# Experts in two parts with separate gate and value passes, and a fourth first-round place of 64 tokens

## The chip, the core and the metric

The kernel runs on one core of one Trainium2 chip. The metric is the device time of one execution in microseconds, as the median of several runs; lower is better. The instructions of PE (matmuls), ACT, DVE, POOL and SP (which here only issues DMAs) run side by side and wait for each other by semaphores.

## What is computed

A two-layer backbone over 256 latent tokens and 256 context tokens, with 1024 channels, all in float32. The last sub-layer, which the change touches, is a top-2-of-8 expert SwiGLU with 3584 hidden columns for each expert:

```python
logits = jnp.einsum('btd,de->bte', h, router_w)
top_vals, top_idx = lax.top_k(logits, 2)
gates = jax.nn.softmax(top_vals, axis=-1)
for e in range(8):
    g, u = jnp.split(h @ w_in[e], 2, axis=-1)
    out = out + combine[..., e:e + 1] * ((jax.nn.silu(g) * u) @ w_out[e])
```

`w_in[e]` is 1024 x 7168 and `w_out[e]` is 3584 x 1024. A row of `w_in` in memory is 28 KB: 14 KB of gate columns, then 14 KB of value columns. The weights of one expert are 42 MiB, those of all eight 336 MiB, and each is read once.

## The kernel before

Everything up to the router is left as it is by the change. The expert stage is `experts(rnd)` in each engine's program. `rnd` 0 is the round that always runs. It takes the experts one after the other at eight places; a place has room for 96 tokens (`CAP`), or for 64 (`SMALL`) at the places in `SMALL_PLACES`. DVE's `expert_order` ranks the experts by their number of tokens, expert 0 always counts as the fullest and stands at place 0, and the least loaded stand at the small places. If an expert has more tokens than its place holds, `overflow_flag` sets a flag, and rounds 1 and 2 run as well, each over all eight experts.

**Blocks and the ring.** SP's `fetch` brings the weights in blocks of 1 MiB, in the order of the list `ROUND`, into a ring of 18 slots (`RING0`). SP issues block n when PE has counted block n - 18 as used (`used`). All transfers stand in one queue. An expert is cut into four steps over its hidden columns, `WIDTH = [1024, 1024, 1024, 512]`. A block of an input step holds, for 128 of the 1024 input rows, 1024 gate and 1024 value columns: two rows of 4 KB in each partition. The fourth step's input blocks hold two times 128 input rows with 512 gate and 512 value columns, in two DMAs: rows of 2 KB. A block of an output step has 256 rows of `w_out`, which lie one behind the other: 8 KB for each partition (in the fourth step two rows of 4 KB). So an expert is 24 input blocks of 4 KB rows, 4 of 2 KB rows, 12 output blocks of 8 KB rows and 2 of 4 KB rows, 42 in all. The list interleaves them: input step s, output step s - 1, and so on, with the first input step of the next expert ahead of the last output step.

**PE.** `in_block` holds the tokens of one input slice as weights, 32 tokens in each of the array's four column groups, and streams the block's columns through; the array's four groups work side by side. With 96 tokens the three groups of 32 tokens take three column groups, and the fourth takes a share of the other columns, so that a 1 MiB block is 12 quarter-array matmuls of 512 columns' worth. With 64 tokens it is 8. The program has one line for most of these matmuls, L1141. Between blocks PE also does `transposes` (of the activated hidden values, 128 x 128 each, L1636 to L1648), `gather` (the next expert's tokens by a one-hot product), `combine` (the last expert's rows back to their tokens) and a transpose of the one-hot (L1707).

**ACT and DVE.** After each input step ACT's `silu` reads the gate from PSUM bank 0 (and a share of bank 2), DVE's `product` multiplies by the value of bank 1, PE transposes the result, and ACT's `transposed` copies the transposed values to SBUF for the output blocks. `hte` copies the gathered tokens, `yhi` and `ylo` split an expert's result for the combining product, `accumulate` adds it up.

The rule for an input block, and what the transfer of a block waits for:

```python
if s_ < STEPS - 1:
    rows = expert_in_w[0, e, b * P:(b + 1) * P, :].rearrange("p (u n) -> p u n", u=2)
    sp.dma_start(w, rows[:, :, 1024 * s_:1024 * s_ + 1024]).then_inc(done, 16)
...
sp.wait_ge(used, B_MOE + n - RING0 + 1)
```

Of the kernel before, what the change touches and what calls it, by code (L numbers as in the profile page):

```python
# [39 lines left out]
SMALL_PLACES = (1, 4, 7)  # L40
N_SMALL = len(SMALL_PLACES)
STEPS = 4
WIDTH = [1024, 1024, 1024, 512]
# [23 lines left out]
def step_blocks(kind, s_, ahead=0):  # L67
    return [(kind, s_, b, ahead) for b in range(WIDTH[s_] // (128 if kind == "in" else 256))]


HEAD = step_blocks("in", 0)
LAST = []
for s_ in range(1, STEPS):
    LAST += step_blocks("in", s_) + step_blocks("out", s_ - 1)
CYCLE = LAST + step_blocks("in", 0, 1) + step_blocks("out", STEPS - 1)
LAST = LAST + step_blocks("out", STEPS - 1)
EB = len(CYCLE)
ROUND = HEAD + CYCLE * (NE - 1) + LAST
assert EB % RING == 0 and len(ROUND) == NE * EB
# [4 lines left out]
def capacity(rnd, e):  # L84

    return SMALL if rnd == 0 and e in SMALL_PLACES else CAP

# [67 lines left out]
def backbone(nc, x, c, ctx_in, c_ctx, ada_w, ada_b, norm_g, mix_in_w, mix_out_w, win_sink, diff_qkv_w,  # L155
# [52 lines left out]
    def area(*specs):  # L208
# [14 lines left out]
    (WMOE, HTE, YS, PTR, YACC, ONEHOT, SIL) = area(  # L223
        ("w_moe", [P, 2 * SPL, BLK], F32), ("h_te", [P, DK, CAP], F32), ("y_split", [P, 2, D], F32R),
        ("onehot_t", [P, 2 * P], F32R), ("y_acc", [P, XT, D], F32), ("onehot", [P, XT, CAP], F32),
        ("silu_g", [P, 768], F32))
# [3 lines left out]
    ACTN = RES[:, 3, 0:768]  # L230
# [48 lines left out]
    ACTT = work(10240, 2, 768)  # L279
# [11 lines left out]
    ps = stack.enter_context(nc.psum_tensor("ps", [P, 8, 512], F32))  # L291

# [199 lines left out]

    def slot_of(rnd, n):
        return LATER[n % RING] if rnd else n % RING0
# [9 lines left out]
    def moe_parts(n):  # L504
        return 2 if ROUND[n][:2] == ("in", STEPS - 1) else 1

    def moe_landed(rnd, e, n):

        def count(top, size):
            return sum(16 * moe_parts(m) for m in range(n % size, top, size))  # L510
        if rnd == 0:
            return count(n + 1, RING0)
        first = sum(16 * moe_parts(m) for m in range(slot_of(rnd, n), len(ROUND), RING0))
        return first + (rnd - 1) * count(len(ROUND), RING) + \
            e * (count(8 + 2 * EB, RING) - count(8 + EB, RING)) + count(n + 1, RING)

    def moe_view(rnd, n):

        kind, s_ = ROUND[n][:2]
        w = ring(slot_of(rnd, n))  # L520
        if kind == "out":
            return w.rearrange("p (j n) -> p j n", j=2)
        if s_ < STEPS - 1:
            return w.rearrange("p (u n) -> p u n", u=2)
        return w.rearrange("p (k u n) -> p k u n", k=2, u=2)
# [11 lines left out]
    def _(sp):  # L537
# [29 lines left out]
        def fetch(rnd, e, n, order=None):  # L567

            kind, s_, b, ahead = ROUND[n]
            w, done = moe_view(rnd, n), w_landed[slot_of(rnd, n)]  # L570
            e = e + ahead if ahead else e
            e = order[e] if order else e
            if kind == "out" and s_ < STEPS - 1:
                rows = expert_out_w[0, e, 1024 * s_ + 256 * b:1024 * s_ + 256 * b + 256, :]
                sp.dma_start(w, rows.rearrange("(p j) n -> p j n", j=2)).then_inc(done, 16)
            elif kind == "out":
                rows = expert_out_w[0, e, 1024 * s_ + 256 * b:1024 * s_ + 256 * b + 256, :]
                sp.dma_start(w, rows.rearrange("(j p) n -> p j n", p=P)).then_inc(done, 16)
            elif s_ < STEPS - 1:
                rows = expert_in_w[0, e, b * P:(b + 1) * P, :].rearrange("p (u n) -> p u n", u=2)  # L580
                sp.dma_start(w, rows[:, :, 1024 * s_:1024 * s_ + 1024]).then_inc(done, 16)
            else:
                for u in range(2):
                    rows = expert_in_w[0, e, 2 * b * P:(2 * b + 2) * P, ED * u + 1024 * s_:ED * u + ED]
                    sp.dma_start(w[:, :, u, :], rows.rearrange("(k p) n -> p k n", p=P)).then_inc(done, 16)  # L585

        def refill(rnd, e, n, turns=0):

            sp.wait_ge(used, moe_base(rnd) + turns * EB + max(n - RING + 1, 0))
            fetch(rnd, e, n)  # L590

        def experts(rnd):
            if rnd == 0:
                for n in [5, 6, 7, 8, 0, 1, 2, 3, 4] + list(range(9, RING0)):
                    if n == 0:
                        sp.wait_ge(scores, U0 + U1)
                    elif n == 3:
                        sp.wait_ge(pv_done, U0 + U1)
                    elif 5 <= n < 5 + RAW:
                        was, j = raw_order[N_RAW - RAW + n - 5]  # L600
                        assert was == "w"
                        sp.wait_ge(lo_done, j + 1)
                    elif n == 5 + RAW:
                        sp.wait_ge(used, B_DOUT + 2)
                    elif n == 7 + RAW:
                        sp.wait_ge(used, B_MOE)
                    elif n == RING0 - 1:
                        sp.wait_ge(hn_done, XT)
                    fetch(0, 0, n)
            else:  # L610
                for n in range(RING):
                    refill(rnd, 0, n)
            if rnd == 0:
                order = [0]
                for n in range(RING0, len(ROUND)):
# [4 lines left out]
                    fetch(0, (n - 8) // EB, n, order)  # L620
                return
            with sp.Fori(0, NE - 2) as e:
                for n in range(RING, EB + 8):
                    refill(rnd, e, n, e)
                for n in range(8, RING):
                    refill(rnd, e + 1, EB + n, e)
            for n in range(RING + EB * (NE - 2), len(ROUND)):
                refill(rnd, (n - 8) // EB, n)
# [88 lines left out]
    def _(act):  # L717
# [310 lines left out]
        def experts(rnd):  # L1028
# [12 lines left out]
            def step_end(s_):  # L1041
                return 8 + max(n for n, x in enumerate(LAST) if x[:2] == ("in", s_)) + 1

            def silu(e, s_, ahead=0):
                J = STEPS * NE * rnd + e * STEPS
                h, q = WIDTH[s_] // 2, WIDTH[s_] // 4
                if s_:
                    act.wait_ge(used, base + e * EB + step_end(s_))
                else:
                    act.wait_ge(used, base + e * EB + 8 - ahead)  # L1050
                act.wait_ge(act_done, FG + J + s_)
                if capacity(rnd, e) == SMALL:
                    act.activation(SIL[:, 0:h], ps[:, 0, 0:h], ACT.Silu).then_inc(silu_done, 1)
                    return
                ins = act.activation(SIL[:, 0:h], ps[:, 0, 0:h], ACT.Silu)  # L1055
                if rnd == 0 and isinstance(e, int) and e + s_ == 0:
                    ins.then_inc(silu_half, 1)
                act.activation(SIL[:, 512:512 + q], ps[:, 2, 0:q], ACT.Silu).then_inc(silu_done, 1)  # L1058

            def transposed(e, s_):  # L1060
                J = STEPS * NE * rnd + e * STEPS
                act.wait_ge(tr_ready, J + (s_ + 1))
                if capacity(rnd, e) == SMALL:
                    n = 4 * P if s_ < STEPS - 1 else 2 * P
                    act.activation(ACTT[:, s_ % 2, 0:n], ps[:, 5, 0:n], ACT.Copy).then_inc(actt_ready, 1)
                elif s_ == STEPS - 1:
                    act.activation(ACTT[:, s_ % 2, 0:384], ps[:, 5, 0:384], ACT.Copy).then_inc(actt_ready, 1)
                else:
                    act.activation(ACTT[:, s_ % 2, 0:512], ps[:, 5, :], ACT.Copy)
                    act.activation(ACTT[:, s_ % 2, 512:768], ps[:, 6, 0:256], ACT.Copy).then_inc(actt_ready, 1)  # L1070

            def yhi(e, last):
                act.wait_ge(used, base + e * EB + 8 + len(LAST if last else CYCLE))
# [6 lines left out]
            def cycle(e, last=False):  # L1080
                transposed(e, 0)
                silu(e, 1)
                transposed(e, 1)
# [3 lines left out]
                silu(e, 2)  # L1087
                transposed(e, 2)
                silu(e, 3)
                if not last:  # L1090
                    hte(NE * rnd + e + 2, capacity(rnd, 0 if rnd else e + 1))
                transposed(e, 3)
# [5 lines left out]
                if not last:  # L1098
                    silu(e + 1, 0, len(step_blocks("out", STEPS - 1)))
# [3 lines left out]
            silu(0, 0)  # L1103
# [35 lines left out]
    def _(pe):  # L1139
# [405 lines left out]
        def in_block(kk, w, width, hold=None):  # L1545

            h, q_ = width // 2, width // 4
            first, last = kk == 0, kk == DK - 1
            for u in range(2):
                if hold:  # L1550
                    hold(u)
                for tg in range(3):
                    mm(ps[group(tg), u, 0:h], HTE[:, kk, group(tg)], w[:, u, 0:h], first, last)
                mm(ps[group(3), u, 0:h], HTE[:, kk, group(0)], w[:, u, h:width], first, last)
            if hold:
                hold(2)
            for u in range(2):
                for n, (tg, c_) in enumerate(QUARTERS):
# [851 lines left out]
```

## Time and profile before

| | |
|---|---|
| median of 3 runs | 1689.19 us (1688.94 to 1690.8) |
| span of the profiled execution | 1685.4 us |
| PE busy in the span | 1612.0 us (96%) |
| DVE, ACT busy | 526.0 us, 400.6 us |
| bytes moved by DMA | 474.61 MB |
| largest group of DMAs | expert weights, 1024.0 KB each |

The profiled execution has no time of its own beside its span; the median lies 3.8 us above the span, and that much is taken to lie around every span of this kernel. The expert stage begins at about 822 us of the span, when PE gathers the first expert's tokens, and goes on to its end. Matmuls are pipelined and their ends are modelled, so a busy PE in a table says little; whether PE waits is read from the chain of waits and from the starts of its matmuls.

### The profile page before, as it was taken

What the parts mean: (1) busy time and instruction counts of PE and PEld (TensorE: products, weight loads), DVE (VectorE), ACT (ScalarE), POOL (GpSimd) and SP (SyncE); (2) the same over time, 40 slices, a digit from 0 to 9 for tenths busy, and PEclk for the clock granted to TensorE, in tenths of its full rate; (3) what the DMA queues carried; (4) which work ended last, traced back from release to release, by engine and by line L of the source; (5) the groups of instructions that cost most, each with busy time, mean ns of one, the idle gap of its engine ahead of it and who ended that gap; (6) DMA issues with size and microseconds to landing.
All of it is one profiled execution on the core that took longest, in us unless ns stands there. A gap on an engine that the chain in (4) does not pass through costs nothing.

```text
span 1685.4 us, 31518 instructions
## 1 busy us (share of the span) xinstructions
PE 1612.0 (96%) x13979; PEld 963.8 (57%) x13979; DVE 526.0 (31%) x829; ACT 400.6 (24%) x724; POOL 34.4 (2%) x70
## 2 busy tenths in 40 slices
PE   5999989999999989998899999999999999999995
PEld 2855778878788877866545334454453444544432
DVE  3427467665433366367400010101101010020012
ACT  3327342222132253357300101011011100010101
POOL 1000100010000000000000000000000000000000
PEclk9999999999999999999899999999999999999998
DMA  9661816576533324214799999999999999999995
GB/s 367 206 225 41 255 45 200 200 254 246 201 100 110 105 79 149 77 50 180 292 376 386 372 409 409 413 406 411 409 408 413 398 411 402 409 412 399 410 400 229
DMA packets 140559, 474.61 MB, mean 282 GB/s; under 512 B 11176, under 2 KB 35144, under 8 KB 121984
## 3 DMA queue, kind: packets, MB, share of 16 engines
q1 hardware_dynamic: 137344, 467.64, 72.9%
q0 software_dynamic: 3072, 4.88, 1.1%
q8 instruction: 112, 1.84, 0.4%
q14 instruction: 31, 0.25, 0.0%
HBM read 471.36 MB, written 1.13 MB: 280 GB/s over the span
## 4 chain that ended last, share of the span: by engine, by line
PE 89%; DVE 4%; DMA 3%; ACT 1%; SPq 1%; issue 1%; DVEq 0%; ACTq 0%
PE ps L1141 86%; DMA w_raw<-in_ada_w_dram 1%; DMA w_moe<-in_expert_out_w_dram 1%; SPq L585 1%; PE ps L1648 1%; PE ps L1324 1%; DVE work L1832 1%; DVE row_max L2100 1%; DVE w_lo L1763 0%; DVE p L2126 0%; PE ps L1640 0%; ACT p L956 0%; DVE h_t L1821 0%; DVE work L2030 0%; PE ps L1485 0%
## 5 line engine op out<-in xcount | busy, mean ns | idle before, releaser
L1141 PE MATMUL ps<-w_hi,h_t 128*128 128x512 f32 (+1 forms) x960 | 294.2, 387 | 11.5 <-DVE h_t L1821 5.4
L1141 PE MATMUL ps<-h_t,w_hi 128*128 128x512 f32 (+1 forms) x768 | 223.1, 375 | 6.2 <-DVE h_t L1821 6.2
L1141 PEld LDWEIGHTS ps<-w_hi,h_t 128*128 128x128 f32 x960 | 180.4, 190 | 48.9 <-DVE w_lo L1946 4.1
L1763 DVE TENSOR_TENSOR w_lo<-w_raw,w_hi 128x2048 fp32r<-128x2048 f32 x57 | 130.5, 2291 | 228.2 <-ACT w_hi L726 227.8
L1141 PE MATMUL ps<-w_lo,h_t 128*128 128x512 f32 (+1 forms) x480 | 185.3, 386 | 0.0
L726 ACT ACTIVATE w_hi<-w_raw 128x2048 fp32r<-128x2048 f32 x57 | 108.9, 1913 | 301.5 <-PE ps L1141 301.3
L1141 PE MATMUL ps<-w_raw,h_te 128*32 128x512 f32 (+2 forms) x2224 | 178.4, 474 | 1.5 <-ACT silu_g L1055 0.8
L1141 PE MATMUL ps<-w_moe,h_te 128*32 128x512 f32 (+2 forms) x2256 | 170.5, 456 | 0.0
L1141 PEld LDWEIGHTS ps<-h_t,w_hi 128*128 128x128 f32 x768 | 141.9, 192 | 33.8 <-issue 9.2
L1141 PE MATMUL ps<-work 128*32 128x512 f32 (+6 forms) x1232 | 147.9, 485 | 6.7 <-ACT p L956 3.7
L2286 DVE TENSOR_TENSOR residual<-silu_g,ps 128x512 f32<-128x512 f32 (+1 forms) x20 | 12.4, 621 | 436.9 <-ACT silu_g L1058 418.0
L1141 PE MATMUL ps<-work,h_te 128*32 128x256 f32 (+1 forms) x1744 | 144.3, 483 | 2.8 <-DMA work<-in_expert_in_w_dram 2.2
L1141 PE MATMUL ps<-h_t,w_lo 128*128 128x512 f32 (+1 forms) x384 | 143.8, 374 | 0.0
L1141 PEld LDWEIGHTS ps<-w_raw,h_te 128*32 128x32 f32 x2224 | 71.0, 110 | 104.8 <-issue 83.8
L1141 PEld LDWEIGHTS ps<-w_moe,h_te 128*32 128x32 f32 x2256 | 71.1, 110 | 91.9 <-issue 71.0
L1055 ACT ACTIVATE silu_g<-ps 128x512 f32<-128x512 f32 (+1 forms) x20 | 10.9, 544 | 398.2 <-PE ps L1141 398.2
L1141 PEld LDWEIGHTS ps<-work,h_te 128*32 128x32 f32 x1744 | 56.0, 110 | 86.1 <-issue 65.0
L1141 PEld LDWEIGHTS ps<-w_lo,h_t 128*128 128x128 f32 x480 | 91.5, 191 | 17.5
L1141 PEld LDWEIGHTS ps<-work 128*32 128x32 f32 (+3 forms) x1232 | 57.8, 126 | 75.3 <-issue 55.0
L1141 PE MATMUL ps<-w_moe,work 128*32 128x512 f32 (+1 forms) x1088 | 94.1, 493 | 0.3 <-DMA w_moe<-in_expert_out_w_dram 0.3
L1141 PE MATMUL ps<-w_raw,work 128*32 128x512 f32 (+1 forms) x832 | 81.4, 532 | 1.4 <-DMA w_raw<-in_expert_out_w_dram 1.3
L1141 PEld LDWEIGHTS ps<-h_t,w_lo 128*128 128x128 f32 x384 | 73.6, 192 | 12.6
(285 smaller groups left out, 1269.9 us busy)
## 6 DMA issues: line engine op xcount, KB each, us to landing
w_raw<-in_expert_in_w_dram SPq DMA_DIRECT2D x68, 1024.0 KB, 18.7
w_moe<-in_expert_in_w_dram SPq DMA_DIRECT2D x62, 1024.0 KB, 18.8
work<-in_expert_in_w_dram SPq DMA_DIRECT2D x53, 1024.0 KB, 18.7
w_raw<-in_ada_w_dram SPq DMA_DIRECT2D x48, 1024.0 KB, 5.6
w_raw<-in_expert_out_w_dram SPq DMA_DIRECT2D x37, 1024.0 KB, 17.9
w_moe<-in_expert_out_w_dram SPq DMA_DIRECT2D x36, 1024.0 KB, 18.0
work<-in_expert_out_w_dram SPq DMA_DIRECT2D x33, 1024.0 KB, 17.7
w_raw<-in_ffn_in_w_dram SPq DMA_DIRECT2D x44, 512.0 KB, 5.0
```

The lines of the kernel that those rows point to most:

```text
L585: sp.dma_start(w[:, :, u, :], rows.rearrange("(k p) n -> p k n", p=P)).then_inc(done, 16)
L726: act.activation(WHI[:, b % SPL, :], WRAW[:, slot_w[b], :], ACT.Copy).then_inc(hi_done, 1)
L1055: ins = act.activation(SIL[:, 0:h], ps[:, 0, 0:h], ACT.Silu)
L1141: return pe.matmul(out_, l, r, start=first, stop=last, skip_group_check=True)
L1324: ins = pe.transpose(ps[:, 4 + kv, c_ * P:(c_ + 1) * P], PR0[:, 2 * (u % 2) + kv, c_ * P:(c_ + 1) * P], ID[:])
L1648: ins = pe.transpose(ps[:, 5 + x // 4, 128 * (x % 4):128 * (x % 4) + 128], pairs[:, x // 2, x % 2, :], ID[:])
L1763: dve.tensor_tensor(WLO[:, b % SPL, :], WRAW[:, slot_w[b], :], WHI[:, b % SPL, :].bitcast(F32), ALU.subtract).then_inc(lo_done, 1)
L1832: ins = dve.tensor_scalar(TF[s][:, n % 2, 256 * k:256 * k + 256], ps[:, UNIT_BANK[s][st][u], 256 * k:256 * k + 256], ACOL[:, st, 2 * u + k ...
L2100: link(dve.tensor_reduce(MX[:, p:p + 2], ps[:, p ^ 2:(p ^ 2) + 2, :], AX_X, ALU.max))
L2286: ins = dve.tensor_tensor(ACTN[:, 0:h], SIL[:, 0:h], ps[:, 1, 0:h], ALU.mult)
```

## The change

An expert is now two parts, A with 2048 hidden columns and B with 1536. The gate columns of a part and its value columns are separate passes (GA, UA, GB, UB), each of eight blocks of 128 input rows: one row of 8 KB for each partition in part A (1 MiB), one of 6 KB in part B (0.75 MiB, which still takes a whole slot of the ring). The output blocks are as before, 8 of part A and 6 of part B; two of these have 4 KB rows where the place has 96 tokens, none where it has 64. So an expert is 46 blocks. The gate pass and the value pass use the same PSUM banks 0 to 2: ACT's `silu` reads the gate out of them before the value pass begins, and DVE's `product` reads the value before the next gate pass. The first-round places with 64 tokens are 1, 3, 5 and 7 instead of 1, 4 and 7. The activated values are multiplied in place, in a tile in `residual`.

```diff
-SMALL_PLACES = (1, 4, 7)
+SMALL_PLACES = (1, 3, 5, 7)
-STEPS = 4
-WIDTH = [1024, 1024, 1024, 512]
+HALVES = ("A", "B")
+WIDTH = {"A": 2048, "B": 1536}
...
+HEAD = in_pass("GA") + in_pass("UA")
+LAST = in_pass("GB") + out_blocks("A", 0, 4) + in_pass("UB") + out_blocks("A", 4, 8)
+CYCLE = LAST + in_pass("GA", 1) + out_blocks("B", 0, 3) + in_pass("UA", 1) + out_blocks("B", 3, 6)
+LAST = LAST + out_blocks("B", 0, 6)
...
-            elif s_ < STEPS - 1:
-                rows = expert_in_w[0, e, b * P:(b + 1) * P, :].rearrange("p (u n) -> p u n", u=2)
-                sp.dma_start(w, rows[:, :, 1024 * s_:1024 * s_ + 1024]).then_inc(done, 16)
...
+                c0 = (0 if what[0] == "G" else ED) + (0 if what[1] == "A" else 2048)
+                sp.dma_start(w, expert_in_w[0, e, b * P:(b + 1) * P, c0:c0 + WIDTH[what[1]]]).then_inc(done, 16)
...
+                n = act_columns(capacity(rnd, e), half)
+                act.activation(SIL[:, 0:n], PSF[:, 0:n], ACT.Silu).then_inc(silu_done, 1)
...
+            for b in range(3):
+                if hold:
+                    hold(b)
+                n = 512 if half == "A" or b < 2 else P
+                for tg in range(3):
+                    piece(tg, b, 0, n, tg, 512 * b)
+                if half == "A":
+                    ins = piece(3, b, 0, 512, b, 1536)
+                elif b == 0:
+                    piece(3, 0, 0, 256, 0, 1280)
+                    piece(3, 0, 256, 256, 1, 1280)
+                elif b == 1:
+                    piece(3, 1, 0, 256, 2, 1280)
+                    piece(3, 1, 256, P, 0, 1152)
+                    piece(3, 1, 384, P, 1, 1152)
+                else:
+                    ins = piece(3, 2, 0, P, 2, 1152)
...
+                if begin and what == "UA":
+                    freed = ((silu_half, 1), (silu_half, 2), (silu_done, FG + 1))
+                    hold = lambda bank: pe.wait_ge(*freed[bank])
...
+                elif b == 0 and what == "GA":
+                    pe.wait_ge(act_done, FG + J + 2 * ahead)
+                elif b == 0 and what == "UA":
+                    pe.wait_ge(silu_done, FG + J + 2 * ahead + 1)
```

SP's queue, in the first expert's last input step, before: rows of four DMAs with two rows of 512 columns in each partition (2 KB each), between output blocks with one row of 2048 (8 KB). `ISA` stands for what SP does for the wait.

```order
L575 DMA w_raw<-in_expert_out_w_dram 128x2048
L585 ISA
L585 DMA w_raw<-in_expert_in_w_dram 128x2x512
L585 ISA
L585 DMA w_raw<-in_expert_in_w_dram 128x2x512
```

Now, at the same place in an expert (the value pass of part B follows the first four output blocks of part A):

```order
L598 DMA w_moe<-in_expert_out_w_dram 128x2048
L601 ISA
L601 DMA w_moe<-in_expert_in_w_dram 128x1536
L601 ISA
L601 DMA w_moe<-in_expert_in_w_dram 128x1536
```

Each input DMA now has one unbroken row for each partition, of 1536 or 2048 columns, where it had two of 512 or 1024.

PE's matmuls of one 1 MiB block of the fourth step before, with 96 tokens (two input slices, each eight matmuls of 256 and eight of 128 columns):

```order
L1141 MATMUL ps<-w_extra,h_te 32x256 x8
L1141 MATMUL ps<-w_extra,h_te 32x128 x8
L1141 MATMUL ps<-w_extra,h_te 32x256 x8
L1141 MATMUL ps<-w_extra,h_te 32x128 x8
L1141 MATMUL ps<-onehot,h_nat 128x64 x16
```

And of one 0.75 MiB block of part B now, with the gather for the next expert behind it:

```order
L1140 MATMUL ps<-w_extra,h_te 32x512 x3
L1140 MATMUL ps<-w_extra,h_te 32x256 x2
L1140 MATMUL ps<-w_extra,h_te 32x512 x3
L1140 MATMUL ps<-w_extra,h_te 32x256
L1140 MATMUL ps<-w_extra,h_te 32x128 x6
L1140 MATMUL ps<-onehot,h_nat 128x64 x16
```

The fourth column group of the array now has two or three shorter matmuls in a row while the other three have one of 512 columns each; before, all four had matmuls of one length in turn.

ACT's first expert before, from the copy of the first transposes on:

```order
L1069 ACTIVATE work<-ps 128x512
L1070 ACTIVATE work<-ps 128x256
L1055 ACTIVATE silu_g<-ps 128x512
L1058 ACTIVATE silu_g<-ps 128x256
L1069 ACTIVATE work<-ps 128x512
L1070 ACTIVATE work<-ps 128x256
L1086 ACTIVATE onehot_t<-ps 96x256
L1055 ACTIVATE silu_g<-ps 128x512
L1058 ACTIVATE silu_g<-ps 128x256
```

And now, from the same copy on:

```order
L1072 ACTIVATE work<-ps 128x1536
L1066 ACTIVATE residual<-ps 128x1152
L1088 ACTIVATE onehot_t<-ps 96x256
L1047 ACTIVATE h_te<-ps,mod_cols,scale_cols 128x64 x8
L1072 ACTIVATE work<-ps 128x1152
L1066 ACTIVATE residual<-ps 128x1024
```

ACT reads up to three banks with one instruction, and has two silus and two copies for each expert where it had four of each.

## Rows read from the trace of the kernel before

**Rows 1.** The page: its first line, and DMA's share and rate in 40 slices.

```profile
span 1685.4 us, 31518 instructions
...
DMA  9661816576533324214799999999999999999995
GB/s 367 206 225 41 255 45 200 200 254 246 201 100 110 105 79 149 77 50 180 292 376 386 372 409 409 413 406 411 409 408 413 398 411 402 409 412 399 410 400 229
```

**Rows 2.** Stretches: busy time of each engine, granted clock, DMA share and rate.

```profile
core 0: us, PE busy (x) PEld busy (x) DVE busy (x) ACT busy (x) POOL busy (x), PEclk, DMA share, GB/s
...
1200.00:1300.00 100.00, 100.00 (x1215) 43.61 (x1211) 9.71 (x20) 10.59 (x26) 0.00 (x0) 1.00 1.02 408
...
940.00:950.00 10.00, 10.00 (x104) 3.19 (x100) 0.00 (x0) 0.00 (x0) 0.00 (x0) 1.00 0.96 370
...
1632.00:1668.00 36.00, 29.97 (x318) 11.09 (x310) 1.19 (x3) 3.05 (x6) 0.00 (x0) 1.00 0.89 350
```

**Rows 3.** PE's timeline, first expert: start us, length us, matmuls (two records each), idle before.

```profile
828.21 13.11 PE L1141 MATMUL ps<-work,h_te 128*32 128x512 f32 x160 [0.52 <-ACT h_te L1035]
841.13 7.92 PE L1141 MATMUL ps<-w_raw,h_te 128*32 128x512 f32 x96
849.86 5.37 PE L1141 MATMUL ps<-w_raw,h_te 128*32 128x512 f32 x64 [0.81 <-ACT silu_g L1055]
855.16 0.98 PE L1648 MATMUL ps<-ident,residual 128*128 128x128 f32 x6
...
871.58 2.76 PE L1141 MATMUL ps<-w_moe,work 128*32 128x512 f32 x32
...
915.18 7.98 PE L1141 MATMUL ps<-w_moe,h_te 128*32 128x256 f32 x192
...
925.70 3.78 PE L1141 MATMUL ps<-onehot,h_nat 128*128 128x64 f32 x32
...
940.37 1.90 PE L1141 MATMUL ps<-work,h_te 128*32 128x512 f32 x16
942.09 3.19 PE L1141 MATMUL ps<-w_raw,h_te 128*32 128x512 f32 x28
```

**Rows 4.** The chain that ended last, 1110 to 1400 us: start us, us, what.

```profile
1134.63 0.48 PE ps L1644 x3
...
1253.09 0.48 PE ps L1644 x3
```

**Rows 5.** The same chain, 1440 to 1460 us.

```profile
1452.93 0.48 PE ps L1644 x3
```

**Rows 6.** The same chain, 1600 us to the end.

```profile
1617.12 8.77 PE ps L1141 x80
...
1647.44 21.01 DMA w_moe<-in_expert_out_w_dram
1668.45 0.04 issue
1668.50 1.97 PE ps L1141 x16
```

**Rows 7.** DMA packets of 1460:1480, 1260:1280, 1160:1180, 1100:1120 us, in this order.

```profile
DMA packets 2109, 8.16 MB, mean 408 GB/s; under 512 B 124, under 2 KB 124, under 8 KB 2107
...
DMA packets 1710, 8.28 MB, mean 414 GB/s; under 512 B 125, under 2 KB 125, under 8 KB 1278
...
DMA packets 1631, 8.26 MB, mean 413 GB/s; under 512 B 125, under 2 KB 125, under 8 KB 1124
...
DMA packets 2153, 8.17 MB, mean 409 GB/s; under 512 B 158, under 2 KB 158, under 8 KB 1639
```

**Rows 8.** DMA packets of 12:24 us, while ada_w comes in 8 KB rows.

```profile
DMA packets 707, 5.10 MB, mean 425 GB/s; under 512 B 85, under 2 KB 85, under 8 KB 85
```

**Rows 9.** SP's DMA queue of 950:1668 us: packets, MB, share of 16 engines.

```profile
q1 hardware_dynamic: 72261, 289.86, 100.9%
```

**Rows 10.** ACT's and DVE's groups by form, 1120 to 1300 us: busy, mean ns, idle.

```profile
L1055 ACT ACTIVATE silu_g<-ps 128x512 f32<-128x512 f32 x3 | 1.8, 597 | 67.5 <-PE ps L1141 67.5
...
L2286 DVE TENSOR_TENSOR residual<-silu_g,ps 128x512 f32<-128x512 f32 x3 | 2.1, 686 | 68.6 <-ACT silu_g L1058 68.6
```

More of the change, by code:

```diff
@@ L1543, in group, with in_block, piece @@
             return slice(GROUP * tg, GROUP * tg + GROUP)
[L1545 to L1549, printed above, removed]
+        def in_block(half, k, w, hold=None):
+            first, last = k == 0, k == DK - 1
+            def piece(q, bank, c0, n, tg, w0):
+                return mm(ps[group(q), bank, c0:c0 + n], HTE[:, k, group(tg)], w[:, w0:w0 + n],
+                          first and c0 == 0, last)
+            for b in range(3):
@@ L1550, in in_block @@
                 if hold:
-                    hold(u)
+                    hold(b)
+                n = 512 if half == "A" or b < 2 else P
                 for tg in range(3):
[L1553 to L1557, printed above, removed]
-                for n, (tg, c_) in enumerate(QUARTERS):
-                    ins = mm(ps[group(n), 2, u * q_:u * q_ + q_], HTE[:, kk, group(tg)],
-                             w[:, u, h + c_ * q_:h + c_ * q_ + q_], first and u == 0, last)
@@ L1575, in out_block @@
-        def out_block(s_, m, w):
-            for j in range(2):
-                first = s_ == 0 and m == 0 and j == 0
-                last = s_ == STEPS - 1 and m == 1 and j == 1
-                for tg in range(3):
-                    mm(ps[group(tg), 3, :], hidden(s_, m, j, tg), w[:, j, 0:512], first, last)
-                mm(ps[group(3), 3, :], hidden(s_, m, j, 0), w[:, j, 512:1024], first, last)
-                for n, (tg, c_) in enumerate(QUARTERS):
-                    ins = mm(ps[group(n), 4, 0:256], hidden(s_, m, j, tg),
+                    piece(tg, b, 0, n, tg, 512 * b)
@@ new lines, in small_hidden, with out_block @@
+        def small_hidden(half, m, j, tg):
+            c_, x = m // (OUTS[half] // 2), m % (OUTS[half] // 2)
+            at = P * (tile_at(SMALL, half) + 2 * x + j) + 32 * (2 * c_ + tg)
+            return ACTT[:, at:at + GROUP]
+        def out_block(half, m, w):
+            for j in range(2):
+                first = half == "A" and m == 0 and j == 0
+                last = half == "B" and m == 5 and j == 1
+                for tg in range(3):
+                    mm(ps[group(tg), 3, :], hidden(half, m, j, tg), w[:, j, 0:512], first, last)
+                mm(ps[group(3), 3, :], hidden(half, m, j, 0), w[:, j, 512:1024], first, last)
+                for n, (tg, c_) in enumerate(QUARTERS):
+                    ins = mm(ps[group(n), 4, 0:256], hidden(half, m, j, tg),
@@ L1598, in small_out_block @@
[L1598 to L1607 removed]
+                    ins = mm(ps[group(n), 3, :], small_hidden(half, m, j, tg), w[:, j, 512 * c_:512 * c_ + 512],
@@ L1688, in cycle @@
+                for n in range(at, len(ROUND) if last else len(HEAD) + EB):
+                    kind, what, b, ahead = ROUND[n]
+                    if (what, b) == ("GA", 0):
                         pe.wait_ge(hte_ready, NE * rnd + e + 2)
-                    if (kind, s_, b) == ("out", 0, 0):
+                    if (what, b) == ("A", 0):
                         pe.wait_ge(acc_done, N * 4 + 1)
-                    product(0 if last else e, n, J, capacity(rnd, 0 if rnd else e + ahead))
-                    if (kind, s_, b) == ("in", 1, 1):
-                        transposes(e, 0)
@@ L1694, in cycle @@
-                    if (kind, s_, b) == ("in", 1, 4) and not (rnd == 0 and at == 8 and e == 0):
+                    product(e, n, capacity(rnd, 0 if rnd else e + ahead))
+                    if (what, b) == ("GB", 1):
+                        transposes(e, "A")
+                    if (what, b) == ("GB", 4) and not (rnd == 0 and not last and e == 0):
                         pe.wait_ge(y_lo, 17 * rnd + e * 2 + 1)
-                        pe.wait_ge(actt_ready, J + 1)
+                        pe.wait_ge(actt_ready, 2 * (NE * rnd + e) + 1)
@@ L1709, in cycle @@
-                    if last and rnd == 0 and (kind, s_, b) == ("out", STEPS - 2, 2):
+                    if (what, b) == ("A", 1):
+                        for t in range(XT):
+                            ins = pe.transpose(ps[0:cap, 7, t * P:(t + 1) * P], ONEHOT[:, t, 0:cap], ID[:])
+                        ins.then_inc(ptt_ready, 1)
+                    if (what, b) == ("UB", DK - 1) and not last:
+                        gather(NE * rnd + e + 2, capacity(rnd, 0 if rnd else e + 1))
+                    if (what, b) == (("A", 5 if early else 7) if last else ("GA", 1)):
+                        transposes(e, "B")
@@ L1710, in cycle @@
+                    if last and rnd == 0 and (what, b) == ("B", 1):
                         pe.wait_ge(gate_row, 1)
@@ L1714, in cycle @@
                         ins.then_inc(gate_spread, 1)
-                    if (kind, s_, b) == ("in", STEPS - 1, 3) and not last:
-                        pe.wait_ge(actt_ready, J + STEPS - 1)
-                        gather(NE * rnd + e + 2, capacity(rnd, 0 if rnd else e + 1))
             if rnd:
@@ L1723, in experts @@
                 pe.wait_ge(hte_ready, NE * rnd + 1)
-            for n in range(8):
-                if rnd == 0:
+            for n in range(len(HEAD)):
+                if rnd == 0 and n < DK:
                     pe.wait_ge(*((hte_first, n + 1) if n < DK - 1 else (hte_ready, 1)))
-                product(0, n, STEPS * NE * rnd, CAP)
+                product(0, n, CAP)
             if rnd:
```

349 lines of the change are left out of this document (149 added, 200 removed).

## The prediction, made before the changed kernel ran

> **What bounds the kernel now.** I read the page's slices first. From slice 21 on, the expert stage, DMA's share is 9 in every slice but the last, at around 408 GB/s [rows 1], and the table of stretches puts it at 1.02 of sixteen engines [rows 2]. PE reads as 100% busy there too, but ends of matmuls are modelled, so that settles nothing. The chain of waits does: from 828 us it goes along PE alone to 1617 and a little beyond, with no wait for a landing; then it turns to SP and the DMA queue, and the last block's landing at 1668.45 starts the last matmuls at 1668.50 [rows 3, 4, 6]. So both run nearly level. PE paces the stage until some 40 us before its end, the queue paces the rest, and the queue had been full all along. Whoever makes only PE faster gains nothing: the last landing stays at 1668.45.
>
> The queue's own account: in 950 to 1668 us it moved 289.86 MB, or 276.4 MiB [rows 9], so 59.6 of the 336 MiB were in at 950. In 940 to 950 it moved 370 GB/s, 3.5 MiB [rows 2]; at 940.37, when PE begins block 40 (the second expert's first, 64 tokens, [rows 3]), 56.1 MiB were in. Slots allow 58 at that moment. A block is thus in about 1.9 blocks, or 4.9 us, after its slot comes free. From there the queue never lacks a slot for long: block 57 is in at about 945.3, and the other 278 MiB take until 1668.45, 723.2 us, which is 109.25 us for an expert's 42 MiB.
>
> **What a packet costs.** Packets are as long as the rows. In 20 us sixteen engines have 320 us; I charge markers and instruction fetches to the data packets [rows 7]. The first stretch has 1983 packets of 4 KB: 0.1614 us each. The second has 1153 of 4 KB and 430 of 8 KB (two fetches taken off): (320 - 186.1) / 430 = 0.311; the third 999 and 505: 0.314; I take 0.313. The fourth has 512 of 8 KB and, by its bytes, 444 of 4 KB and 1037 of 2 KB: 0.0849. A packet costs some 0.01 us beside its bytes, so longer rows are cheaper for the byte. For 6 KB no row exists; it lies between 0.0849 + 0.1614 = 0.246 (cut in two) and 0.75 x 0.309 = 0.232, and I take the middle of 4 and 8 KB, 0.2372. That 8 KB rows with a gap between them (here 28 KB apart) go as fast as the unbroken output blocks is borne out by `ada_w`, whose 8 KB rows lie 24 KB apart: 622 packets in 192 engine-microseconds, 0.309, at 425 GB/s [rows 8].
>
> **The change part by part.** *Rows of the transfers.* Before, an expert is 6656 packets of 4 KB, 2048 of 2 KB and 1536 of 8 KB: 1074.3 + 173.9 + 480.8 = 1729.0, over 16 engines 108.06 us. The queue needed 109.25, 1.1% more. Now, with 96 tokens: 3584 of 8 KB, 2048 of 6 KB, 512 of 4 KB: 1121.8 + 485.8 + 82.6 = 1690.2, or 105.64 us; with 64 tokens 3840 and 2048: 105.48. With the same 1.1%, 106.7 us an expert: 2.5 us less for each.
>
> *The ring.* A 0.75 MiB block takes a whole slot, so the ring holds fewer bytes. PE begins block 16 at 871.58 before [rows 3]. Now blocks 0 to 15 are again of 1 MiB and 2.58 us (841.13 - 828.21 over five, [rows 3]). Blocks 16 to 18 are of part B, whose 96-token matmuls are three quarters of the columns, 1.94 us; with 12 transposes (0.92 us for six, so 1.84) block 18 is done at about 879.3. From there PE frees slots of 0.75 MiB every 1.94 us, and what is fetched into them is soon 1 MiB at 2.5 us: the queue is the slower one from block 36 on, where it was so only from block 57 before. Block 36 is in 4.9 us later, at 884.2, with 16 + 6 + 4 + 6 + 1 = 33 MiB. The other 303 MiB take 303 / 42 x 106.7 = 769.8: the last landing at 1654.0 instead of 1668.45. Of the 18 us that the rates would give, 4 go to the ring.
>
> *PE.* A cycle with 96 tokens takes 118.46 us (1134.63 to 1253.09, [rows 4]), one with 64 tokens beside one with 96 together 199.84 (1253.09 to 1452.93, [rows 4, 5]), so 81.4. The fourth small place replaces 118.5 by 81.4, 37 us of PE. Transposes are as many for a 96-token expert and cost some 0.5 us less in two sets than in four. PE now needs about 828.2 + 4 x 199 = 1624 without waits (some 4 less, since the last cycle has no gather), 30 before the last landing. So the fourth place gives nothing by itself: the work it removes is hidden behind the queue. Without it PE would need 37 more, 1661 less 4, about level with the queue.
>
> *New waits.* In the first expert UA follows GA directly and GB follows UA, in the same banks; each waits for one bank's silu or product, 0.81 us as at block 8 before [rows 3]. One of the two is new; the six transposes that stood before block 16, 0.92 us [rows 3], are gone from there, so block 16 keeps its 871.58. In the later experts at least three output blocks (5.2 us with 64 tokens) lie between the passes, over a silu or a product of 1536 columns, at most three times 0.6 or 0.69 us [rows 10]. PE's gather (3.7 us, [rows 3]) is followed by four output blocks, as before. Had a wait of 3 us for each pair of experts no cover, PE's 199 stay under the queue's 213.4. Blocks 0 and 1 now use slots that SP fills later, but all slots stood filled or issued before 828. The tail behind the last landing is the same.
>
> *The sum.* 1668.45 - 1654.0 = 14.5 us less. The span goes from 1685.4 to 1670.9, and with the 3.8 us around it the time is 1674.7; I say 1674.5.
>
> **A rule against it.** The stretches of 2, 4 and 8 KB rows differ in cost for the byte by 8% [rows 7]. The Trainium skill's page "DMA: Bandwidth & Descriptors" (Specifications) puts the least transfer for line rate at 512 B. By that, rows of 2 to 8 KB would all go at one rate, and the first rival below would be the outcome. The trace speaks against it within this range.
>
> **The rivals.** *One rate for all rows: slower.* If input rows of 8 and 6 KB, 28 KB apart, go at the rate of 4 KB rows, only the ring's smaller content is left: 303 MiB at 109.25 / 42 from 884.2 end at 1672.4, 4 us later than now, time 1693. It decides where an expert takes more than 108.7 us. Against it: [rows 8]. 6%.
>
> *Part B's matmuls do not pack.* The fourth column group has two or three matmuls in a row beside one in the others. If the others wait, a block costs up to 512 + 256, 512 + 256 and 128 column turns instead of 1152: about 2.8 us, 13.7 more in a 96-token expert. PE's pair then needs 213, as much as the queue's, and PE ends near 1624 + 55 - 4 = 1675, 4 us behind its end now (1670.47, [rows 6]): time 1693. The nearest row is the fourth step's, with 128- and 256-column matmuls at 2.63 us a MiB [rows 3], no dearer, but of equal lengths. It matters from about 2.4 us a block. 6%.
>
> *More than that: 8 KB rows at 0.309 and fewer fetches.* With [rows 8]'s price all through, an expert takes 104.3; with the 1.1% it is 105.4, the last landing at 1645, time 1665; without it 1657. 9%.
>
> *The clock.* Once small experts wait for the queue, PE works 1.72 us (942.09 - 940.37, [rows 3]) of each 2.5. If the granted clock fell to 1.2 GHz there, a block would take 3.44 us, over the queue's pace, and each such expert 50 us more: about 1775. Sixteen such MiB undo the gain. But in 1632 to 1668 us PE waited just so, for the same blocks, and the clock stood at 1.00 [rows 2], 2.4 GHz. The Trainium skill ("TensorE: Matmul & The Clock Gate", HAM oscillation) warns that waits for DMA throttle the array; this stretch does not show it. 3%.
>
> *Overflow.* Routing the reference's inputs gives 58, 55, 70, 77, 62, 65, 62, 63 tokens. Expert 0 is kept out; the four least of the rest, 55, 62, 62, 63, fit into 64. Were the fourth over 64, two more rounds of eight experts at 107 us would run, 1700 us. 2%.
>
> **How the numbers follow.** The forecast itself: 74%, between 1667 and 1682 (an expert at 105.5 to 108 us). The range takes part of the faster rival and reaches toward the slower two: 1664 to 1684.5. A change under 0.2%, 3.4 us, is about what a measurement cannot tell from none. Faster: 74 + 9 = 83%. A few of each rival that ends near 1693 fall within 0.2% (1692.6): 5%. Slower: 12%.
>
> **What will show it.** Stretches of GA and UA transfers should run at 415 to 420 GB/s, an expert's 44 MB should take 106.7 us, the chain should turn to the DMA queue near 1200 us and not at 1620, and PE should stand idle in the small experts while its clock stays 1.00. Part B blocks should start 1.94 us apart with 96 tokens. The last landing should be at 1654 and 17 us before the span's end. I would be wrong if the rate stays at 408, if blocks of part B take over 2.4 us, or if matmuls double in length behind waits.

## The result, and the profile after

| | before | after |
|---|---|---|
| median, four runs each on one chip | 1689.71 us | 1673.07 us (1671.87 to 1674.8) |
| ratio | 1 | 0.9903, 95% interval 0.9891 to 0.9914 |
| profiled execution: span, own time | 1685.4 us, not known | 1670.0 us, 1671.87 us |

The change makes the kernel 16.6 us faster in the medians and 15.4 in the profiled spans. 1674.5 was predicted, with a range of 1664 to 1684.5. All ratios leave out runs over 1.5% above the fastest of the same kernel, as a slow state; there were two, both of e6_two_dmas.

The page of the changed kernel, its span, DMA's share and rate in 40 slices, the packets and the chain by engine:

```profile
span 1670.0 us, 28575 instructions
...
DMA  9661816676523323213699999999999999999995
GB/s 368 210 226 36 258 51 202 199 256 231 217 85 120 117 82 126 101 51 138 253 318 390 417 418 421 417 419 418 418 421 418 419 418 418 420 418 419 418 418 213
DMA packets 106754, 474.42 MB, mean 284 GB/s; under 512 B 11176, under 2 KB 35144, under 8 KB 70784
...
PE 64%; SPq 19%; DMA 9%; DVE 5%; issue 2%; ACT 1%; DVEq 0%; ACTq 0%
```

Against [rows 1] the share in the expert stage still reads 9, in every slice but the last, and only the rate shows the change: from slice 24 on, but for the last, it is 417 to 421 GB/s where it wandered between 398 and 413. The digit says that the queue is never empty, not how fast it is. The chain that ends last now turns to the queue after two fifths of the stage, and from there on changes between the queue (SPq is SP's sequencer, which issues the transfers; DMA is a block under way) and PE. Its pieces from 1132 us on (start us, us, what):

```profile
1132.68 1.25 PE ps L1654 x9
1133.92 10.48 PE ps L1140 x96
1144.56 2.00 SPq L601
...
1242.07 26.44 DMA work<-in_expert_out_w_dram
1268.55 1.92 PE ps L1140 x16
1270.52 4.11 PE ps L1140 x36
...
1627.61 26.15 DMA w_raw<-in_expert_out_w_dram
1653.76 0.04 issue
1653.80 1.97 PE ps L1140 x16
```

In [rows 4] PE stood alone in it. The last landing was at 1668.45 [rows 6] and is at 1653.76. PE's waits, from 1140 to 1654 us (what waits for what, us in total, times, longest):

```profile
PE ps L1140 <- DMA w_raw<-in_expert_in_w_dram: 6.1, 14, 0.6
PE ps L1140 <- DMA work<-in_expert_out_w_dram: 5.0, 10, 0.7
PE ps L1140 <- DMA w_moe<-in_expert_in_w_dram: 4.4, 12, 0.4
PE ps L1140 <- DMA w_raw<-in_expert_out_w_dram: 3.0, 6, 0.6
```

They are many and short, nearly all of the small places' blocks; the longest one, a block of output weights in `w_moe`, is 1.0 us. And two stretches of the new kernel (the columns are those of [rows 2]), the second with a small place in it; PE is not quite full and its clock is:

```profile
1200.00:1300.00 100.00, 98.79 (x1024) 43.34 (x1020) 7.60 (x12) 9.10 (x15) 0.00 (x0) 1.00 1.01 419
...
1340.00:1440.00 100.00, 92.09 (x912) 32.71 (x908) 8.87 (x16) 9.43 (x19) 0.00 (x0) 1.00 1.01 418
```

### The profile page after: what moved, and what is told of

Same layout as the page of the kernel before. It is cut to its first block, busy times and chain, and to the rows that moved or that the text cites. A ratio compares the mean times of both kernels' runs of the same rounds, so it can differ in the third digit from the quotient of the medians.

```text
span 1670.0 us, 28575 instructions
## 1 busy us (share of the span) xinstructions
PE 1583.0 (95%) x12596; PEld 953.8 (57%) x12596; DVE 519.8 (31%) x791; ACT 391.1 (23%) x655; POOL 34.5 (2%) x70
## 4 chain that ended last, share of the span: by engine, by line
PE 64%; SPq 19%; DMA 9%; DVE 5%; issue 2%; ACT 1%; DVEq 0%; ACTq 0%
PE ps L1140 62%; SPq L601 13%; SPq L598 6%; DMA w_moe<-in_expert_out_w_dram 2%; DMA work<-in_expert_out_w_dram 2%; DMA w_raw<-in_expert_out_w_dram 2%; DMA work<-in_expert_in_w_dram 1%; DMA w_raw<-in_ada_w_dram 1%; DMA w_moe<-in_expert_in_w_dram 1%; PE ps L1323 1%; DVE work L1835 1%; PE ps L1654 1%; DVE row_max L2103 1%; DVE w_lo L1766 0%; SPq L596 0%
## 5 line engine op out<-in xcount | busy, mean ns | idle before, releaser
L2290 DVE TENSOR_TENSOR residual<-residual,ps 128x1152 f32<-128x1152 f32 (+3 forms) x15 | 19.4, 1292 | 529.1 <-PE ps L1140 529.1
L1140 PE MATMUL ps<-w_raw,h_te 128*32 128x512 f32 (+2 forms) x1694 | 159.5, 519 | 7.0 <-DMA w_raw<-in_expert_in_w_dram 6.1
L1140 PE MATMUL ps<-work 128*32 128x512 f32 (+6 forms) x1104 | 141.9, 498 | 11.4 <-DMA work<-in_expert_out_w_dram 5.0
L1140 PE MATMUL ps<-work,h_te 128*32 128x512 f32 (+2 forms) x1662 | 147.4, 506 | 0.9 <-ACT h_te L1047 0.5
L1140 PEld LDWEIGHTS ps<-w_raw,h_te 128*32 128x32 f32 x1694 | 61.3, 110 | 98.9 <-issue 70.2
L1140 PEld LDWEIGHTS ps<-work,h_te 128*32 128x32 f32 x1662 | 65.6, 110 | 78.8 <-issue 61.7
L1140 PEld LDWEIGHTS ps<-work 128*32 128x32 f32 (+3 forms) x1104 | 53.4, 128 | 79.0 <-issue 52.2
L1140 PE MATMUL ps<-w_raw,work 128*32 128x512 f32 (+1 forms) x1024 | 93.8, 513 | 3.0 <-DMA w_raw<-in_expert_out_w_dram 3.0
L1140 PE MATMUL ps<-w_moe,work 128*32 128x512 f32 (+1 forms) x832 | 76.2, 515 | 1.6 <-DMA w_moe<-in_expert_out_w_dram 1.6
L1140 PEld LDWEIGHTS ps<-w_raw,work 128*32 128x32 f32 x1024 | 34.3, 110 | 58.7 <-issue 42.9
```

Source lines behind the costliest of these rows:

```text
L1140: return pe.matmul(out_, l, r, start=first, stop=last, skip_group_check=True)
L2290: dve.tensor_tensor(SIL[:, 0:n], SIL[:, 0:n], PSF[:, 0:n], ALU.mult).then_inc(act_done, 1)
```

## The experiments

Eight kernels ran, each against the kernel before on its own chip. The ratio to the kernel before is what I compare: 0.001 of it is 1.7 us. The expert stage starts up to 5 us earlier or later in one profiled execution than in another, so places in two traces are compared after taking off that shift, read from one row: the start of the matmuls of block 8, behind the hold for ACT, at 850.09 in the changed kernel.

### Part A's rows cut in two (e4_cut_a), then both parts' (e3_cut_both)

```diff
-                sp.dma_start(w, expert_in_w[0, e, b * P:(b + 1) * P, c0:c0 + WIDTH[what[1]]]).then_inc(done, 16)
+                c1 = {'A': c0, 'B': min(c0, 5120)}[what[1]]
+                half = WIDTH[what[1]] // 2
+                if what[1] in 'A':          # 'AB' in e3_cut_both
+                    rows = expert_in_w[0, e, b * P:(b + 1) * P, c1:c1 + 2 * (half + 256)].rearrange('p (u n) -> p u n', u=2)
+                    sp.dma_start(w.rearrange('p (u n) -> p u n', u=2), rows[:, :, 0:half]).then_inc(done, 16)
```

Blocks, bytes, slots, order and matmuls stay; only the packets are shorter, with 1 KB left out between the two pieces of a row. So these kernels read some other hidden columns than the reference. The places of the tokens are settled before these rows are used, so the work stays the same.

> As the kernel with both parts cut, but only part A's rows come in two pieces of 4 KB; part B keeps its rows of 6 KB. The wrong hidden columns are read in part A. Theory: 16 blocks of an expert cost 2.56 us instead of 2.48 or 2.49, the last landing is at 1661 to 1662 and the time 1681, 8 us over the changed kernel. Rival (rows of 6 KB are what matters, or neither): 1673 to 1675.

> The changed kernel, but each input block's rows come in two pieces with a gap of 256 columns in the source: 2 x 4 KB in part A, 2 x 3 KB in part B. Same bytes, same number of DMAs, same PE work; the wrong hidden columns are read, so this part of the computation is changed. Theory (a packet has a fixed cost beside its bytes): an expert takes 109.3 us of the queue, the last landing is at 1671 to 1673 and the time 1691 to 1693, which is slower than the kernel before by 2 to 4 us, because the ring holds fewer bytes. Rival (the gain comes from fewer passes, fewer DMAs or less PE work, not from the rows): it stays at 1673.

Measured: part A cut, 1680.54 us, ratio 0.9956 (0.994 to 0.9971). Both cut, 1690.81 us, ratio 1.0009 (1.0 to 1.0018). From 0.9903 that is 9.0 us for part A and 9.0 more for part B, each give or take some 3 by the intervals. The first came out as expected, the second 0.2 us under its range. In the traces, put on one start, the last landing comes 9.0 us later with part A cut and 15.7 with both, so the rows are worth 16 to 18 us. With both cut, all the rest of the change is in place and the gain is gone. One stretch of the kernel with both cut, packets:

```profile
DMA packets 1956, 8.20 MB, mean 410 GB/s; under 512 B 125, under 2 KB 125, under 8 KB 1789
```

That is 1330 to 1350 us. And of the changed kernel 1310 to 1330 us, where nearly every row has 8 KB, and 1507 to 1521 us, where most have 6 KB:

```profile
DMA packets 1146, 8.37 MB, mean 419 GB/s; under 512 B 126, under 2 KB 126, under 8 KB 126
...
DMA packets 970, 5.85 MB, mean 418 GB/s; under 512 B 107, under 2 KB 107, under 8 KB 710
```

In 20 us sixteen engines have 320 us; without markers and two fetches the first row leaves 1018 packets, 0.314 us each. In the second, 14 us are 224 engine-microseconds; 258 packets of 8 KB at 0.313 take 81, and 603 of 6 KB the other 143: 0.2375 us each. The prediction had 0.313 and 0.2372. The gain is the length of the rows, and the first rival (one rate for all, 1693) is about what the cut kernel shows: 1690.8.

### Two DMAs for a block, by columns (e8_two_cols) and by partitions (e6_two_dmas)

A cut row also has another address pattern. So another kernel gets 4 KB rows in part A from two DMAs of 1024 columns each, and a further one has two DMAs with whole rows, each of 64 partitions:

```diff
+                if what[1] == "A":      # e8_two_cols
+                    for c1 in (0, 1024):
+                        sp.dma_start(w[:, c1:c1 + 1024], expert_in_w[0, e, b * P:(b + 1) * P, c0 + c1:c0 + c1 + 1024]).then_inc(done, 16)
...
+                if what[1] == "A":      # e6_two_dmas
+                    for p0 in (0, 64):
+                        sp.dma_start(w[p0:p0 + 64, :], expert_in_w[0, e, b * P + p0:b * P + p0 + 64, c0:c1]).then_inc(done, 16)
```

The second ran first:

> The changed kernel with each block of part A in two DMAs of 64 partitions, rows of 8 KB as before: 16 DMAs more for an expert, the same packets. Theory (packets cost, DMAs don't): within 1.5 us of the changed kernel. Rival (the number of DMAs counts, as with the fourth step's pairs before the change): 5 us or more slower.

Measured: 2017.06 us in the median of all four runs (1990.64 to 2051.51); the ratio of the two fastest is 1.1842 (1.1777 to 1.1907). The theory is refuted. The rival has the sign, but neither foresaw the size. The runs lie 3% apart, so the size is rough. In the stretch 1330 to 1350 us, while blocks of part A come in:

```profile
DMA  9999997999997999999999999999999999999999
GB/s 434 385 274 209 209 238 193 258 242 209 225 176 160 254 225 258 258 209 242 221 225 209 262 213 213 213 246 213 213 246 213 246 180 229 213 213 246 213 213 246
DMA packets 702, 4.67 MB, mean 234 GB/s; under 512 B 126, under 2 KB 126, under 8 KB 153
```

The rate falls from some 420 to 220 GB/s while all engines stay busy. Without markers and the fetch, 548 packets of 8 KB and 27 of 6 KB fill 320 us: some 0.57 us for one of 8 KB, where a DMA over 128 partitions has 0.314 for the same packet. Either the 64 partitions or the further DMAs could do that, so:

> Blocks of part A are brought by two DMAs, each over all 128 partitions and half of the columns (rows of 4 KB, 0.5 MiB a DMA); the rest is as in the changed kernel, and the result is the reference's. The kernel with part A's rows cut inside one DMA has the very same packets (1680.5 us measured, last landing 8.3 us later than with whole rows). Theory (what counts is the length of the packets, a DMA's own cost being hidden by the others in the queue): 1680 to 1682 us, landings of part A's blocks 2.56 us apart. Rival (each further DMA in the queue costs something of its own, and this is what made the kernel with two DMAs of 64 partitions 340 us slower): that one had 128 DMAs more in the round, so 2.7 us for each; this kernel then has 128 more as well and takes about 2020 us. In between, 0.1 us for each DMA would be 13 us, about 1693.

Measured: 1680.89 us (1680.41 to 1681.56), ratio 0.9946 (0.9929 to 0.9962), against 0.9956 for the rows cut inside one DMA. Its rate in the same stretch:

```profile
DMA packets 1907, 8.24 MB, mean 412 GB/s; under 512 B 210, under 2 KB 210, under 8 KB 1597
```

With as many DMAs as the slow kernel it loses only what 4 KB rows lose. So 128 further DMAs in a full queue cost nothing that can be measured (the two ratios are known to some 2.5 us), and the price is that of the 64 partitions. The Trainium skill's page "SBUF — State Buffer" (Door 1: The DMA port swizzle) says that a transfer to 64 partitions reaches only half of SBUF's ports, and (Can I just issue two DMAs to hit both halves?) that a second DMA on the other half does not make up for it; this trace agrees, with 220 GB/s of 420.

### Two slots of the ring taken away (e5_ring16)

```diff
+FIRST = 16
-                for n in range(RING0, len(ROUND)):
+                for n in range(FIRST, len(ROUND)):
-                    sp.wait_ge(used, B_MOE + n - RING0 + 1)
+                    sp.wait_ge(used, B_MOE + n - FIRST + 1)
```

> The changed kernel with 16 slots of the ring in the first round instead of 18; all else as it is. Theory (the ring's bytes at the moment when the queue becomes the slower one are a head start, and are paid for one by one): the last landing moves by 4.5 us to 1658, the time to 1677.5. Rival (the queue is full whatever the ring holds): within 1 us of the changed kernel. Other rival (the ring is now so short that landings come too late in the 96-token experts, again and again): 10 us or more slower.

Measured: 1677.76 us, ratio 0.9931 (0.9915 to 0.9948): 4.7 us more than the changed kernel, as expected. The rate is the same, 419 GB/s in 1200 to 1300 us; what is lost lies ahead of that. Up to 828 us, on one start, its queue had moved 131.03 MB and that of the changed kernel 132.60; up to 950 us the gap is 1.7 MB, or 4 us of the queue. Here a ring that holds less loses the missing content once, and no more. This is the mechanism of the prediction's 4 us for slots that are only three quarters full. It was shown with whole slots; a ring with unused space put to use wasn't tried.

### The small places (e1_three_small, e7_two_small, e2_before_four)

```diff
-SMALL_PLACES = (1, 3, 5, 7)
+SMALL_PLACES = (1, 4, 7)      # e1_three_small; (3, 7) in e7_two_small
```

and in the kernel before (e2_before_four) the reverse, (1, 3, 5, 7) instead of (1, 4, 7).

> The kernel before with the small places 1, 3, 5 and 7; nothing else. Theory: the last landing stays within 1 us of 1668.5 and the time at 1689, since the queue has held every block's landing back all along; only PE idles earlier. Rival (PE paces the stage): 10 us or more faster, 1679 or less.

> The changed kernel with the small places 1, 4 and 7, as before the change; nothing else. Theory (the DMA queue bounds the stage from block 36 on, and PE has 30 us to spare): PE does 37 us more and nothing moves; last landing at 1653.8 us, time 1673, within 2 us of the changed kernel. Rival (the fourth small place brings the gain, since PE paces the stage): the time comes back by 10 us or more, to 1683 to 1690.

> The changed kernel with only two small places, 3 and 7. It marks the point at which PE takes over. Theory: PE needs 74 us more than with four, 1694 us without waits less what the queue hides: PE's last block ends near 1692 and the time is 1708 to 1712, 36 us over the changed kernel, while three and four small places are alike. Rival (PE has more to spare than that): under 1690.

Measured: the kernel before with four places 1687.78 us, ratio 0.999 (0.9981 to 0.9999): 1.7 us less by the ratio (0.2 to 3.2), 0.75 by the medians, since the queue paces it. PE had 37 us less to do and waited for landings instead, 32 us from 1140 to 1672 us where it was 6 before. The changed kernel with three 1677.97, ratio 0.9936 (0.9922 to 0.9949), 5.6 us more than with four, where at most 2 were expected. With two 1716.08, ratio 1.016 (1.0143 to 1.0177), where 1708 to 1712 was expected: 43 us more than with four, not 36. Both miss to the same side, by 4 to 7 us. With three places PE waits for no landing at all; its wait table from 1140 to 1665 us has one line:

```profile
PE ps L1140 <- DVE y_split L2263: 1.5, 1, 1.5
```

Its chain goes along PE. The transposes of part A of three experts (start us, us, what), with one place of 64 tokens between the first two and none between the others:

```profile
1192.85 1.64 PE ps L1654 x12
...
1392.06 1.63 PE ps L1654 x12
...
1510.28 1.64 PE ps L1654 x12
```

A 96-token cycle takes 118.22 us, and the small place adds 199.21 - 118.22 = 81.0: a small place saves 37.2 us of PE. And the end of the stage, PE's timeline (columns of [rows 3]), the kernel with three places first, the changed kernel behind it:

```profile
1653.58 2.05 PE L1140 MATMUL ps<-mod_rows,ident 8*128 8x128 f32 x16
1655.55 1.92 PE L1140 MATMUL ps<-work 128*32 128x512 f32 x16
1657.30 5.33 PE L1140 MATMUL ps<-w_raw,work 128*32 128x512 f32 x48
1664.12 2.38 PE L1140 MATMUL ps<-y_split,onehot_t 64*128 64x512 f32 x8 [1.50 <-DVE y_split L2263]
```

```profile
1645.78 2.05 PE L1140 MATMUL ps<-mod_rows,ident 8*128 8x128 f32 x16
1647.76 1.92 PE L1140 MATMUL ps<-work 128*32 128x512 f32 x16
1649.50 3.77 PE L1140 MATMUL ps<-w_raw,work 128*32 128x512 f32 x32
1653.80 1.92 PE L1140 MATMUL ps<-w_raw,work 128*32 128x512 f32 x16 [0.54 <-DMA w_raw<-in_expert_out_w_dram]
1657.22 2.38 PE L1140 MATMUL ps<-y_split,onehot_t 64*128 64x512 f32 x8 [1.50 <-DVE y_split L2263]
```

The last blocks end at 1662.63 and about 1655.8. The stage began 1.63 us later in the first (its block 8 at 851.72), so PE without the fourth place ends at 1661.0 of the changed kernel's time, 5.2 behind the end that the queue sets. With two places (block 8 at 853.28) the last row (`y_split`) is at 1702.93, or 1699.74 after the same correction; that is 37.2 behind the one of three places (1662.49), the price of a place once more.

## Why the prediction was right, step by step

**What bounds the kernel, right.** The queue did. The kernel before with four small places shows it from PE's side: 37 us less work for PE, 0.75 to 1.7 us less time, and waits for landings in its place.

**The price of the rows, right, and the whole of the gain.** 0.314 and 0.2375 us for 8 and 6 KB rows, and 16 to 18 us back when the rows are cut. From 884 to 1654 us the queue moved:

```profile
q1 hardware_dynamic: 48687, 317.68, 99.8%
```

317.68 MB are 303.0 MiB, which is what the prediction left to be moved from 884.2 on, in 769.8 us; 42 MiB thus take 106.7 us. The last landing came at 1653.76 for 1654.0. The 1.1% that was carried over without an explanation held as well, and this is in part luck. It is some 8 us here. About 6 of them are the end of the queue, where the share stands at a half (last section), and nearly all the rest is 0.314 in place of 0.313. In the kernel before that end costs only about 3 of its 8 us, and what the other 5 are stays open.

**The ring, right.** The queue's step (884.2, 33 MiB in) is confirmed by the same row, and two slots less cost 4.7 us.

**PE, right, but for the fourth place.** In the first expert:

```profile
850.09 7.93 PE L1140 MATMUL ps<-w_raw,h_te 128*32 128x512 f32 x72 [0.81 <-ACT residual L1062]
857.82 13.08 PE L1140 MATMUL ps<-w_moe,h_te 128*32 128x512 f32 x120
871.87 2.16 PE L1140 MATMUL ps<-w_moe,h_te 128*32 128x512 f32 x30 [0.97 <-DVE residual L2287]
873.80 2.18 PE L1140 MATMUL ps<-w_extra,h_te 128*32 128x512 f32 x30
875.91 1.70 PE L1654 MATMUL ps<-ident,residual 128*128 128x128 f32 x12
877.54 9.96 PE L1140 MATMUL ps<-work,h_te 128*32 128x512 f32 x150
887.24 2.11 PE L1140 MATMUL ps<-w_raw,h_te 128*32 128x512 f32 x29
```

Block 16 starts at 871.87 (predicted 871.58), the new hold is 0.97 (0.81), and five blocks of part B take 887.24 - 877.54, 1.94 us each, as predicted: the matmuls of unlike lengths pack, and that rival is out. A pair of experts takes 199.2 (199). The sentence "the fourth place gives nothing by itself" is the step that failed. The sum behind it, 1661 without the place, is what the kernel with three places shows, 1661.0. What was wrong is the "less 4" for the missing gather of the last cycle. By the measured cycles, three pairs of 199.21 and two of 118.22 from 828.5 on end at 1662.5; PE ended at 1661.0, so the two ends of the stage save 1.5 us and not 4. The last cycle has 2.05 us of other matmuls (`mod_rows`, in the trace of before too, and not counted), and the first expert has its two holds, 0.81 and 0.97; how the rest divides no run here takes apart. The remaining 1.4 us lie in the start and in the rounded cycles. The sum (1657) was then called "about level with the queue", while its end had to be held against the end of the last block, 1655.8. The fourth place is worth 5.6 us in this kernel and nearly nothing in the kernel before, whose queue ends 15 us later: with three places 10.8 us of the gain are left (ratio 0.9936).

**The clock, right.** It stands at 1.00 where PE waits for its blocks. The waits there are at most 1.0 us; in the kernel with two DMAs of 64 partitions they were longer, and the clock wasn't spared (below).

**The chain, right in the main.** It turns to SP and the queue at 1144 us, 56 us ahead of the 1200 predicted, and then changes between the queue and PE.

**What lies around the span, half right.** The profiled execution of the changed kernel has a time of its own, 1671.87 us, so 1.9 us lie around its span and not 3.8. The other 1.2 to the median are the difference between executions; the prediction's 3.8 held both. What follows the last landing is 16.2 us long, for 17.0 before.

Taken one at a time from the changed kernel, row length is worth 16 to 18 us, and the fourth place 5.6. They don't add up to the gain: the fourth place is worth its 5.6 only behind the longer rows, and the ring takes some 4 us away.

## What to carry to other kernels

When a full DMA queue paces a kernel, count its packets and not only its bytes: rows of 8 and 6 KB instead of 4 and 2 gave 2% of the queue's time here (109.25 to 106.7 us for an expert) and 1% of the kernel's, at the price of another order of the matmuls and some 4 us for slots that aren't full. A busy share of 9 in every slice says that the queue is full, and the rate beside it whether it could be faster. An edit that is worth nothing alone can be worth something behind another one: work out the second resource's own end to the last instruction, and hold it against the same instruction of the first.

## What was not expected of the hardware

**Sixteen engines that don't end together.** The packets of the last blocks, changed kernel, 1620 to 1655 us (share and rate in 40 slices of 0.875 us):

```profile
DMA  9999999999999999999999965555555654543100
GB/s 403 419 417 421 407 431 412 433 421 414 440 412 431 403 440 393 403 431 412 412 440 412 403 290 234 243 243 243 225 234 234 262 197 197 215 206 150 66 0 0
```

At 1640 us the share falls to a half, and stays there for 13 us. All blocks had been issued by 1628, so this is read as half of the engines having done their part of the last blocks, and the other half being behind by the time of five blocks. The kernel before, 1635 to 1670 us:

```profile
DMA  9999678999999999999999999999996555442000
```

Here that stretch is some 6 us long. In the kernel with two small places, which PE paces, the share falls from 9 to 2 within 4 us. If the work of the last 13 us were even over all engines, the last landing would come about 6 us earlier, as an estimate from these shares. The Trainium skill's page "DMA: Bandwidth & Descriptors" (The descriptor swizzle) says that in a transfer to 128 partitions engines 0 to 7 serve partitions 0 to 63 and 8 to 15 the others; half of the engines running behind would fit with that, but the profile doesn't name the engine of a packet, and why one half is slower stays open.

**A starved PE at a lower clock.** Stretches of the kernel with two DMAs of 64 partitions (columns of [rows 2]):

```profile
1330.00:1350.00 20.00, 12.59 (x128) 5.96 (x120) 0.95 (x1) 2.24 (x8) 0.00 (x0) 1.00 1.02 234
1400.00:1500.00 100.00, 80.03 (x837) 35.12 (x833) 6.64 (x11) 5.59 (x6) 0.00 (x0) 0.95 0.92 297
1200.00:1300.00 100.00, 63.59 (x497) 17.15 (x493) 1.22 (x1) 2.52 (x3) 0.00 (x0) 0.85 1.02 274
1500.00:1600.00 100.00, 65.76 (x561) 23.68 (x552) 1.35 (x1) 4.62 (x10) 0.00 (x0) 0.88 0.93 222
```

In the last three PE waited 12 to 20 times in 100 us, for up to 3.9 us at a time, and the granted clock is 0.85 to 0.95, so in part of the time it was at 1.2 instead of 2.4 GHz. A block that started at 1231.59 took 3.41 us, the one at 1236.28 took 1.92. The first stretch, with waits of 2.1 to 2.4 us and PE busy for 12.6 of 20, still has 1.00, so waits of that length didn't bring the clock down there. In the changed kernel, with waits of up to 1.0 us, it stayed at 1.00. So the rival "the clock falls" has its condition in a queue at half its rate, and not in waits as short as the changed kernel's. The Trainium skill's page "TensorE: Matmul & The Clock Gate" (HAM oscillation) describes a clock that falls at waits for DMA, there of some 3 to 5 us; this trace agrees that it falls, but already at shorter waits: those from 1203 to 1222 us, in which it went from 1.00 to 0.84, were 1.2 to 2.8 us long. What it cost the kernel can't be read apart, since the queue paced these stretches.
